# Two attentions on one core: one group of dense products goes from a pair's slot 18 to its slot 2, and the keys' factor is widened one slot later

## The reference, cut to what matters

```python
# first block: dilated attention, three patterns mixed by their denominators, with ALiBi penalties
proj = rmsnorm(x, g_norm) @ w_in            # q, k, v and a gate come out of this product
y_b = dilated_attention(q, k, v) * silu(b_gate)
...
# second block: stick-breaking attention
k = rmsnorm_2(kv[..., :SB_WIDTH].reshape(bsz, s, SB_HEADS, SB_HEAD_DIM), k_g)   # kv = rmsnorm(h) @ w_kv
q = rmsnorm_2(qg[..., :SB_WIDTH].reshape(...), q_g)                               # qg = rmsnorm(h) @ w_in
z = einsum('bhtd,bhsd->bhts', q[:, :, q0:kend], k[:, :, :kend])
log_keep = where(strict, log_sigmoid(-z), 0.0)
suffix = cumsum(log_keep, reverse=True) - log_keep
weights = where(strict, exp(log_sigmoid(z) + suffix), 0.0)
out = weights @ v[:, :, :kend]
...
y = (o * silu(gate)) @ w_out
```

## Time and profile before

| | us |
|---|---|
| median of three executions | 3143.16 |
| lowest and highest | 3139.32 and 3149.51 |
| profiled execution | 3143.99 |
| its span from the first to the last instruction | 3142.5 |
| TensorE busy in the span | 3046.1 (97%) |
| VectorE busy | 1841.0 (59%) |
| ScalarE busy | 1394.8 (44%) |
| GpSimd busy | 660.4 (21%) |

### The profile page before, as it was taken

The page is one execution under the profiler, slowest core; times in us unless marked ns, Lnnn a source line. Parts: engine busy times, 40 slices in busy tenths (PEclk is TensorE's granted clock), DMA queues, the critical chain, the costliest instruction groups (busy, mean ns, idle before and its releaser), DMA issues. The chain is left out here.

```text
span 3142.5 us, 39543 instructions
## 1 busy us (share of the span) xinstructions
PE 3046.1 (97%) x15324; PEld 2542.7 (81%) x15324; DVE 1841.0 (59%) x2502; ACT 1394.8 (44%) x2104; POOL 660.4 (21%) x444
## 2 busy tenths in 40 slices
PE   8999999999999999999999999998999999998998
PEld 7888888888888878787877877777878888886787
DVE  4444223666676534377667566676557777776544
ACT  5333213555555423335244252443346666666531
POOL 1210002222222100302010020110234445444210
PEclk9999999999999999999999999999999999998999
DMA  3111222212111234112121121211121111112422
GB/s 110 52 46 49 73 71 70 69 54 61 54 61 61 87 115 150 47 36 81 41 74 54 41 81 47 68 54 60 34 101 41 41 41 41 41 41 74 154 100 75
DMA packets 58808, 208.44 MB, mean 66 GB/s; under 512 B 6929, under 2 KB 9873, under 8 KB 58513
## 3 DMA queue, kind: packets, MB, share of 16 engines
q1 hardware_dynamic: 49360, 174.16, 16.6%
q0 software_dynamic: 9280, 31.99, 3.3%
HBM read 170.87 MB, written 26.87 MB: 63 GB/s over the span
## 5 line engine op out<-in xcount | busy, mean ns | idle before, releaser
L119 ACT ACTIVATE whi<-wraw 128x1024 fp32r<-128x1024 f32 x208 | 218.4, 1050 | 416.0 <-PE a_D L132 64.2
L124 DVE TENSOR_TENSOR wlo<-wraw,whi 128x1024 fp32r<-128x1024 f32 x173 | 237.9, 1375 | 156.3 <-ACT whi L119 155.2
L130 PE MATMUL ssm_D<-x1hi,whi 128*128 128x512 f32 x640 | 257.6, 403 | 2.1 <-issue 2.1
L130 PE MATMUL b_D<-x1hi,whi 128*128 128x512 f32 x640 | 254.1, 397 | 0.9 <-DVE wlo L124 0.9
L132 PE MATMUL ssm_D<-x1hi,wlo 128*128 128x512 f32 x640 | 250.4, 391 | 0.0
L131 PE MATMUL ssm_D<-x1lo,whi 128*128 128x512 f32 x640 | 250.1, 391 | 0.0
L132 PE MATMUL b_D<-x1hi,wlo 128*128 128x512 f32 x640 | 250.0, 391 | 0.0
L131 PE MATMUL b_D<-x1lo,whi 128*128 128x512 f32 x640 | 249.8, 390 | 0.0
L2643 DVE TENSOR_TENSOR_SCAN stick_keep<-stick_keep,stick_first 128x896 f32<-128x896 f32 (+7 forms) x128 | 215.0, 1684 | 43.3 <-ACT stick_keep L2530 42.9
L2795 POOL TENSOR_TENSOR stick_rows<-stick_rows,stick_keep 128x896 f32<-128x896 f32 (+7 forms) x128 | 162.1, 1269 | 261.9 <-DVE stick_keep L2643 248.1
L130 PE MATMUL a_D<-x1hi,whi 128*128 128x512 f32 x512 | 201.9, 394 | 11.6 <-DVE x1lo L159 11.6
(11 more groups left out here) (458 smaller groups left out, 7684.0 us busy)
## 6 DMA issues: line engine op xcount, KB each, us to landing
wraw<-w_dram SPq DMA_DIRECT2D x208, 512.0 KB, 3.6
sq<-acum_rows SPq DMA_DIRECT2D x32, 512.0 KB, 3.8
att_bias<-alibi_dram SPq DMA_DIRECT2D x16, 512.0 KB, 3.9
stack<-stack POOLq DMA_DIRECT2D x32, 256.0 KB, 3.7
f<-y_b SPq DMA_DIRECT2D x11, 512.0 KB, 6.0
x_sb<-xT_dram SPq DMA_DIRECT2D x8, 512.0 KB, 7.9
branch_a<-sq POOLq DMA_DIRECT2D x8, 512.0 KB, 3.5
y_b<-att_y POOLq DMA_DIRECT2D x8, 512.0 KB, 3.0
```

The costliest lines, as they stand in the source:

```text
L119: act.activation(self.whi[:, s, :, :], self.wraw[:, s, :, :], ACT.Copy).then_inc(self.w_hi, 1)
L124: dve.tensor_tensor(self.wlo[:, s, :, :], self.wraw[:, s, :, :], self.whi[:, s, :, :].bitcast(F32), ALU.subtract).then_inc(self.w_lo, 1)
L130: pe.matmul(out, self.whi[:, s, w0, :], xhi[:, k, cols], start=start, stop=False)
```

## The change

One unit goes from slot 18 to slot 2 in both attentions, since they share the table, and three steps of the second attention's keys go one slot later.

```diff
-UNITS = [4, 4, 4, 3, 2, 4, 4, 3, 3, 3, 3, 2, 2, 4, 4, 3, 4, 4, 4]
+UNITS = [4, 4, 5, 3, 2, 4, 4, 3, 3, 3, 3, 2, 2, 4, 4, 3, 4, 4, 3]
...
-AUX_SLOT = dict(k_square=5, k_sum=6, k_wide=7, k_spread0=8, k_spread1=9, v_turn0=12, v_turn1=13, k_parts=11, k_low=17,
+AUX_SLOT = dict(k_square=5, k_sum=6, k_wide=8, k_spread0=9, k_spread1=10, v_turn0=12, v_turn1=13, k_parts=11, k_low=17,
                 q_parts=16, q_square=16, q_sum=17)
```

## The result

| | us |
|---|---|
| median after (3185.89 to 3190.96) | 3188.25 |
| median before, in the same comparison | 3143.65 |
| ratio, 95% interval | 1.0143 (1.0129 to 1.0157) |
| profiled execution after, its span | 3187.2, 3185.7 |

The change makes the kernel 1.4% slower: 43.2 us in the profiled executions (3187.2 against 3143.99), where 34.9 had been forecast. TensorE's clock over the span is 0.987, before 0.989.

What follows compares the result with a forecast made beforehand. TensorE was taken as the bound nearly everywhere, an edit paying only where it waits. First attention +11.1 and second +23.8 make +34.9 on 3143.99: 3178.9, for the median 3178; 8-in-10 range 3156 to 3192.

Steps and rivals of the forecast that it cites:

- the clock: Rival: new gaps in slots 5 and 10 bring half-rate stretches, at most 1.7 each, up to 3202; above 3190, chance 0.10.
- crossing: From one pair of the second attention to the next, the shorter slot 18 gains 0.5 us, seven times: -3.5.
- 1.58 a pair: First attention, slot 5: ScalarE's moved split and copies delay the next score by 1.58 us, seven pairs: +11.1.
- TensorE never waits there: First attention, from slot 6 on: no TensorE waits, so nothing gives back the 1.58 us a pair.
- It ends at 2583.53 + 1.09: Second attention, slots 4 and 5: VectorE's split waits for GpSimd and ends 1.09 us after it, at 2584.62.
- 1.4 to 1.9 ... I take 1.6: Second attention, slots 5 and 6: new loss per pair, 1.9 if slot 6's running product goes before GpSimd's block.
- A gap of 2.5: Second attention, slot 10: TensorE waits 2.5 us for the weights' low part; loss taken as 2.3 a pair.
- a short old wait in slot 11 takes some back: Second attention, slot 11: an old wait absorbs some of four transposes' 0.44 us; loss taken as 2.3 (2.0 to 2.5).
- Costs nothing there: Second attention, slot 2: the unit's 0.69 us fits into TensorE's 0.99 us wait and adds nothing.
- The rivals (a) to (c): (a) only slot 2's wait: 3139.7, 0.04; (b) only first attention: 3150.8, 0.06; (c) splits beside GpSimd: 3162, or between, 0.10.

Runs made afterwards that it cites:

- the kernels with only that wait: Unit moved, only the second attention's values' steps following, against the kernel before; keys' factor later: 3166.62, ratio 1.0069; factor in old slots: 3165.76, ratio 1.0064.
- the unit alone: Kernel before with the unit in slot 2, VectorE's and ScalarE's orders and the keys' factor as before: 3142.71, ratio 0.9994.
- a wait of 0.8: Kernel with the values' steps moved and the old factor slots, GpSimd weighing only 128 of 1024 columns of slot 9's block: 3143.67, ratio 0.9993 against the kernel before.
- slot 5's wait of 1.3 alone: Kernel before with the unit in slot 2 and only the second attention's keys' steps moved along, factor in old slots: 3157.1, ratio 1.0037.
- the kernel with the factor alone: Kernel before with only the keys' factor one slot later, the unit where it was: 3148.0, ratio 1.0009.

## Why the prediction was right, and where it was too small

The direction and the mechanism were right, 3178 was 10 too low, and 3188 lies inside the range, in part by luck (see the clock). The terms, worked out from the starts of the slots' scores in the two profiled executions:

| term | forecast | measured |
|---|---|---|
| first attention, 7 pairs | +11.1 | +11.2 |
| second, slots 5 and 6 | +11.2 | +13.5 |
| second, slots 8 to 11 | +16.1 | +18.4 |
| second, crossing and slots 0 to 3 | -3.5 | -2.6 |
| second, two falls of the clock (+2.1), pair 4's slots 5 to 7 (-0.3) | 0 | +1.8 |
| between the two attentions | 0 | +2.6 |
| last pair and rest | 0 | -1.7 |
| sum | +34.9 | +43.2 |

**First attention.** 1.58 a pair was forecast, 1.60 came, in slot 5 (3.93 to 5.55) where it was expected. The last pair has the split and not the copies, and its slot 5 stays at 3.93: a split of 1.05 fits the cover, as forecast. "TensorE never waits there", said of the slots from 6 on, isn't so: it waits 0.66 in slot 16 of seven pairs. But that wait is 0.66 before and after, so it gave nothing back.

**Slots 5 and 6.** The step "It ends at 2583.53 + 1.09" held to 0.01 (1.08 after GpSimd's end). The undersized term is "1.4 to 1.9 ... I take 1.6": 2.03 came. Slot 6's running product went ahead of GpSimd's block, the case that the text had left open and priced at 1.9; and a stop costs more than the late start. TensorE's last product before it started at 2527.50, so the next was due at 2527.73; it started at 2529.16, 1.43 later (1.4 was forecast), and the one behind it 0.22 after it instead of 0.12. An idle time that the list gives as 1.27 lengthened the slot by 1.54.

**Slots 9 and 10.** A gap of 2.5 was forecast and 2.29 came, with 0.27 for the stop beside it. The step that failed is "a short old wait in slot 11 takes some back": with the factor one slot later it takes nothing back (slot 11 stays at 3.87), without it 0.5. Nor is the later factor free as a whole: it costs 0.23 a pair alone and 0.56 here.

**The crossing.** -0.5 was forecast, -0.38 came: slots 15 to 18 gain 0.39, slots 0 and 1 0.31, and slot 2 loses 0.35, since its wait fell only from 0.99 to 0.66. "Costs nothing there" was too kind: the turn at its end still waits for GpSimd.

**The clock.** It was a rival with one chance in ten, and it came in part: two of the changed kernel's seven pairs have a fall behind slot 10's wait, 1.05 each. In the kernels with only that wait five of seven had one. With seven it would by estimate have stood 5 x 1.05 higher, at about 3193, just above the range: that the time stayed inside it is luck, as nothing in the prediction says which pairs fall.

**The rivals (a) to (c)** fall: the unit alone gives 77.70 a pair, but only with the old orders; both attentions lose, each by itself; and the splits don't run beside GpSimd (2.73 against 1.22).

## What to carry to other kernels

Where one table places work on the bottleneck engine and also decides when other engines follow, count the edit on each engine's queue, and separate the two if the follower has no reason to move: here the unit by itself did no harm, and its followers cost 1.4%. Put an early step of another engine behind what the bottleneck waits for, not ahead of it, unless the row of the timeline shows more cover than its duration. Price a VectorE instruction on two SBUF operands with GpSimd's work beside it, and a stop of TensorE with its restart.

## What the runs showed that was not expected

- The half-rate stretches behind slot 10's wait don't come in every pair: with the same wait of 2.3 in all seven pairs, five had one in two kernels and two in the changed kernel, by one profile each; with a wait of 0.8 none had. With slot 5's wait of 1.3 alone two pairs had one, but later, in slot 7; whether that wait brings them isn't shown. What picks the pairs isn't settled.
- The Trainium skill, "TensorE: Matmul & The Clock Gate", section "HAM oscillation — how this bites in real kernels", tells of falls from a wait ahead of every tile. The rows agree in kind: behind a wait of 2.3 the granted clock was 0.50 over 3.4 us, in a part of the pairs.
- The stretch from the first attention's last pair to the second's first score has the same work in every kernel, but for one unit's place; it took 1303.22 before, 1305.80 after and 1311.29 in the kernel with the factor alone, which leaves that place too as it was, with a granted clock of 0.99, 0.99 and 0.98. A single profile can't tell gains of a few microseconds in total; the length of a pair, which repeats to a few hundredths, can.
